# Seven of 22 gate and up pairs as seven block products, three-pass scores in the mLSTM, and another order in the banded attention

## The reference, cut to what matters

```python
def swiglu(x, wg, wu, wd):
    return (jax.nn.silu(x @ wg) * (x @ wu)) @ wd
```

```python
wts = jnp.exp(dmat - m_out[..., None])          # dmat holds a triangular mask
s_qk = jnp.einsum('bhcjd,bhcsd->bhcjs', q, k) * wts
num = jnp.einsum('bhcjs,bhcsv->bhcjv', s_qk, v) + ...
```

```python
s = s - slopes[:, :, None, None] * dist
pe = jnp.exp(s - m)
attn = pe / (jnp.sum(pe, axis=-1, keepdims=True) + jnp.exp(sink_l - m))
```

## Time and profile before

| | us |
|---|---|
| median of 3 runs | 3383.4 |
| lowest and highest run | 3382.89, 3386.52 |
| profiled execution | 3386.68 |
| its span on the core | 3384.6 |
| TensorE busy in it | 3327.2 |
| VectorE, ScalarE, GpSimd busy | 1828.3, 1315.1, 17.3 |

### The profile page before, as it was taken

One profiled execution on the slowest core, in us unless ns is written; L12 is line 12 of the kernel. 1 busy time (PEld: TensorE's weight loads), 2 busy tenths in 40 slices (PEclk: granted clock), 3 DMA queues, 4 the chain that ended last, 5 costly groups with the idle time before them and its releaser, 6 DMA issues.

```text
span 3384.6 us, 42860 instructions
## 1 busy us (share of the span) xinstructions
PE 3327.2 (98%) x17260; PEld 2783.2 (82%) x17260; DVE 1828.3 (54%) x2976; ACT 1315.1 (39%) x2272; POOL 17.3 (1%) x53
## 2 busy tenths in 40 slices
PE   8999999999999999999999999999999999999998
PEld 7778888888878888888888778888888888788887
DVE  5777974434886543354436367443554337674446
ACT  4554442223574322242224445222342226653233
POOL 0000000000100000000000000000000000000000
PEclk9999999999999999999999999999999999999999
DMA  3313122233201322323232202323232332023244
GB/s 139 100 57 102 63 83 98 98 102 97 88 15 63 104 96 100 106 94 99 94 106 95 81 32 82 100 95 105 94 100 94 100 106 72 32 82 107 99 143 168
DMA packets 95640, 311.94 MB, mean 92 GB/s; under 512 B 17167, under 2 KB 18709, under 8 KB 95445
## 3 DMA queue, kind: packets, MB, share of 16 engines
q1 hardware_dynamic: 92600, 305.51, 27.2%
q10 hardware_dynamic: 2844, 3.71, 0.3%
HBM read 302.88 MB, written 2.10 MB: 90 GB/s over the span
## 4 chain that ended last, share of the span: by engine, by line
PE 89%; DVE 6%; ACT 3%; issue 1%; DMA 0%; SPq 0%; DVEq 0%; ACTq 0%
PE ps L303 25%; PE ps L305 25%; PE ps L304 25%; PE ps L300 13%; DVE WL L293 1%; ACT WH L287 1%; DVE R L694 1%; DVE XL L869 0%; DVE XT L860 0%; PE ps L3137 0%; DVE XT L863 0%; ACT XH L631 0%; ACT R L629 0%; DVE S L707 0%; PE ps L2392 0%
## 5 line engine op out<-in xcount | busy, mean ns | idle before, releaser
L303 PE MATMUL ps<-XH,WH 128*128 128x512 f32 (+1 forms) x3200 | 1186.4, 371 | 19.5 <-DVE XL L869 12.1
L305 PE MATMUL ps<-XH,WL 128*128 128x512 f32 (+1 forms) x3200 | 1170.9, 366 | 0.0
L304 PE MATMUL ps<-XL,WH 128*128 128x512 f32 (+1 forms) x3200 | 1170.8, 366 | 0.0
L293 DVE TENSOR_TENSOR WL<-RAW,WH 128x1024 fp32r<-128x1024 f32 x567 | 686.2, 1224 | 287.3 <-ACT WH L287 282.8
L303 PEld LDWEIGHTS ps<-XH,WH 128*128 128x128 f32 x3200 | 606.8, 190 | 124.9 <-DVE XL L869 11.4
L305 PEld LDWEIGHTS ps<-XH,WL 128*128 128x128 f32 x3200 | 606.5, 190 | 97.4
L304 PEld LDWEIGHTS ps<-XL,WH 128*128 128x128 f32 x3200 | 607.3, 190 | 93.8 <-issue 0.2
L287 ACT ACTIVATE WH<-RAW 128x1024 fp32r<-128x1024 f32 x567 | 587.3, 1050 | 144.9 <-DMA RAW<-units 91.5
L303 PE MATMUL ps<-HH,WH 128*128 128x512 f32 (+1 forms) x990 | 362.7, 366 | 0.0
L304 PE MATMUL ps<-HL,WH 128*128 128x512 f32 (+1 forms) x990 | 361.8, 365 | 0.0
L305 PE MATMUL ps<-HH,WL 128*128 128x512 f32 (+1 forms) x990 | 361.7, 365 | 0.0
(11 more groups left out here) (596 smaller groups left out, 3221.4 us busy)
## 6 DMA issues: line engine op xcount, KB each, us to landing
RAW<-units SPq DMA_DIRECT2D x567, 512.0 KB, 3.3
da_qx<-da_qs SPq DMA_DIRECT2D x64, 64.0 KB, 2.4
XIN<-in_x ACTq DMA_DIRECT2D x2, 1024.0 KB, 6.3
out<-YT SPq DMA_DIRECT2D x8, 256.0 KB, 3.2
mb_pairf<-constants ACTq DMA_DIRECT2D x1, 512.0 KB
GB<-in_ln_g SPq DMA_DIRECT2D x1, 512.0 KB
GB<-in_ln_b SPq DMA_DIRECT2D x1, 512.0 KB
da_pi<-in_positions ACTq DMA_DIRECT2D x1, 256.0 KB, 2.9
```

The source lines that it names most:

```text
L293: nc.vector.tensor_tensor(WL[:, u % RING, :], RAW[:, u % RING, :], WH[:, u % RING, :].bitcast(F32), ALU.subtract)\
L303: nc.tensor.matmul(out, wh, xh, start=start, stop=False)
L304: nc.tensor.matmul(out, wh, xl, start=False, stop=False)
L305: return nc.tensor.matmul(out, wl, xh, start=False, stop=stop)
```

## The change: what it does

**Feed-forward.** For the pairs j = 5 to 11 of every feed-forward (`SEVEN`), the two units and the activations are seen as 2 x 2 blocks: gate and up columns, two halves of 512 input rows, two halves of 256 tokens. Seven block products (Strassen's method in Winograd's form) take the place of eight. Each is four row tiles x three matmuls of 256 tokens:

```diff
+        def seven_pe(pe, e, j):
+            ...
+            pe.wait_ge(S["sums_split"], halved(s))
+            part_pe(X, plain(u, 0), block(0, 0), True).then_inc(S["parts_done"], 1)
+            part_pe(Y, wsum(0), xsum(0), True).then_inc(S["parts_done"], 1)
+            pe.wait_ge(S["ffn_act"], kept(f, j, 1))
+            part_pe(X, wsum(1), xsum(1), False).then_inc(S["parts_done"], 1)
+            if j > SEVEN[0]:
+                pe.wait_ge(S["ffn_dve"], joined(f, j - 1, 2))
+            part_pe(Z, plain(u, 4), block(4, 0), True).then_inc(S["unit_done"], 1)
+            pe.wait_ge(S["ffn_act"], kept(f, j, 3))
+            part_pe(X, plain(u + 1, 0), xsum(2), False).then_inc(S["parts_done"], 1)
+            part_pe(Y, wsum(2), block(4, 1), False).then_inc(S["parts_done"], 1)
+            pe.wait_ge(S["ffn_act"], kept(f, j, 4))
+            part_pe(X, plain(u + 1, 4), xsum(3), False).then_inc(S["unit_done"], 1)
```

GpSimd makes the sums. Once for each feed-forward, when all of XH and XL is there, nine operations of 128 x 1024 give four sums of activation blocks; for each of the seven pairs, four operations of 128 x 512 give the sums of the weight blocks. The first of the four goes into the up unit's place in RAW, in place of half of it; the others go to WSR, of which there are two:

```diff
+                for i, j in enumerate(SEVEN):
+                    u, b = e["n0"] + 2 * j, j % 2
+                    for n in (u, u + 1):
+                        pool.wait_ge(raw_in[n % RING], 16 * (n // RING + 1))
+                    if i >= 2:
+                        pool.wait_ge(S["unit_done"], u + 2 - 4)
+                    ...
+                    own(g.tensor_tensor(u1, g1, u1, ALU.subtract), "sums_made")
+                    own(g.tensor_tensor(s2, u2, u1, ALU.subtract), "sums_made")
+                    own(g.tensor_tensor(s4, g2, s2, ALU.subtract), "sums_made")
+                    own(g.tensor_tensor(s1, s2, g1, ALU.add), "sums_made")
```

ScalarE and VectorE split the sums into high and low parts where they split the up unit: 128 x 1536 in one instruction each (`hi_to`, `lo_to`). The weights' low part of a gate unit waits for all four sums of its pair, as it overwrites RAW:

```diff
         def hi_to(act, n):
             for u in range(split["hi"], min(n, n_units)):
-                act.wait_ge(raw_in[u % RING], 16 * (u // RING + 1))
+                s = ups.get(u)
+                if s is None:
+                    act.wait_ge(raw_in[u % RING], 16 * (u // RING + 1))
+                else:
+                    act.wait_ge(S["sums_made"], made(s, 1))
                 nc.scalar.activation(WH[:, u % RING, :], RAW[:, u % RING, :], ACT.Copy).then_inc(S["wh_ready"], 1)
+                if s is not None:
+                    act.wait_ge(S["sums_made"], made(s, 4))
+                    b = SEVEN[s % NS] % 2
+                    nc.scalar.activation(WSH[b][:], WSR[b][:], ACT.Copy).then_inc(S["sums_high"], 1)
```

The units are now split four ahead of a pair instead of five, from pair 3 to pair 11 (`split_at`). The work of ScalarE and VectorE on one of the seven pairs is:

```diff
+                def seven(j):                       # ScalarE
+                    act.wait_ge(S["parts_done"], 5 * s + 1)
+                    nc.scalar.activation(sg[:, 0:HT], ps[:, b, 0:HT], ACT.Copy).then_inc(S["ffn_act"], 1)
+                    hi_to(act, split_at(e, j, 0))
+                    act.wait_ge(S["parts_done"], 5 * s + 2)
+                    nc.scalar.activation(hid[:, HT:T], ps[:, b + 1, 0:HT], ACT.Copy).then_inc(S["ffn_act"], 1)
+                    act.wait_ge(S["parts_done"], 5 * s + 3)
+                    nc.scalar.activation(sg[:, HT:T], ps[:, b, 0:HT], ACT.Copy).then_inc(S["ffn_act"], 1)
+                    hi_to(act, split_at(e, j, 1))
+                    ...
+                def seven(j):                       # VectorE
+                    lo_to(dve, split_at(e, j, 0))
+                    ...
+                    own(v.tensor_tensor(sg[:, 0:HT], sg[:, 0:HT], ps[:, 6, 0:HT], ALU.add), "ffn_dve")
+                    own(v.tensor_tensor(hid[:, HT:T], hid[:, HT:T], hid[:, 0:HT], ALU.add))
+                    own(v.tensor_tensor(sg[:, HT:T], sg[:, HT:T], ps[:, b + 1, 0:HT], ALU.add), "ffn_dve")
+                    own(v.scalar_tensor_tensor(sg, TH[:, j % 2, :], 1.0, sg, ALU.add, ALU.mult))
+                    ...
```

```diff
-            mm(ps[:, KBANK[h][i], :], K[:, h, i * P:(i + 1) * P], Q[:, h, :]).then_inc(s["st"], 1)
+            mm(out, KH[:, h, ts], QH[:, h, :], True, False)
+            mm(out, KH[:, h, ts], low_of(h, 0), False, False)
+            mm(out, low_of(h, 1)[:, ts], QH[:, h, :], False, True).then_inc(s["st"], 1)
...
-            mm(ps[:, 2, :], both, NM[:], True, True)
-            mm(ps[:, 3, :], both, NM[:], True, False)
-            for i in range(TT):
-                last = mm(ps[:, 3, i * P:(i + 1) * P], identr[:], TRI[:, d, :], False, i == 3)
-            last.then_inc(s["sp"], 1)
+            mm(ps[:, 2 + d, :], ROWS[:, row:row + 1].to_broadcast([P, P]), NM[:]).then_inc(s["sp"], 1)
```

More of the change, by code:

```diff
@@ L3296, in dve, with sums, weigh, low @@
         lo_to(dve, nk + 9)
+        def sums(p):
+            dve.wait_ge(s["pr"], 9 * p + 9)
+            own(v.tensor_tensor(RC, L[:, p % 2, :, :], ES[:, p % 2, :, :], ALU.add))
+            own(v.reciprocal(RC, RC))
+        def weigh(p, q):
+            o, _, n = BAND[order[q]]
+            for c in range(2):
+                w = PR[:, p % 2, c, o:o + n * P]
+                own(v.tensor_scalar(w, w, RC[:, q, c:c + 1], None, ALU.mult), "comb", wait=c == 1)
+        def low(p):
+            dve.wait_ge(s["ohi"], p + 1)
+            own(v.tensor_tensor(OL[:, p, :], ps[:, 0, :], OH[:, p, :].bitcast(F32), ALU.subtract), "olo")
         maxima(0, 2)
@@ L3317, in dve @@
-        dve.wait_ge(s["ohi"], NP)
-        own(v.tensor_tensor(OL[:, NP - 1, :], ps[:, 0, :], OH[:, NP - 1, :].bitcast(F32), ALU.subtract), "olo")
+        sums(0)
+        weigh(0, 0)
+        maxima(1, 0)
+        maxima(1, 1)
+        weigh(0, 1)
+        weigh(0, 2)
+        weigh(0, 3)
+        maxima(1, 2)
+        maxima(1, 3)
+        sums(1)
+        lo_to(dve, n2 + 5)
+        weigh(1, 0)
+        weigh(1, 1)
+        low(0)
+        maxima(2, 0)
+        maxima(2, 1)
+        weigh(1, 2)
@@ new lines, in dve @@
+        weigh(1, 3)
+        maxima(2, 2)
+        maxima(2, 3)
+        lo_to(dve, n2 + 6)
+        sums(2)
+        weigh(2, 0)
+        low(1)
+        maxima(3, 0)
+        maxima(3, 1)
+        weigh(2, 1)
+        weigh(2, 2)
+        weigh(2, 3)
+        maxima(3, 2)
+        maxima(3, 3)
+        lo_to(dve, n2 + 7)
+        sums(3)
+        weigh(3, 0)
+        weigh(3, 1)
+        low(2)
+        maxima(4, 0)
+        maxima(4, 1)
+        weigh(3, 2)
+        weigh(3, 3)
+        maxima(4, 2)
@@ new lines, in dve @@
+        maxima(4, 3)
+        lo_to(dve, n2 + 8)
+        sums(4)
+        weigh(4, 0)
+        weigh(4, 1)
+        maxima(5, 0)
+        maxima(5, 1)
+        low(3)
+        weigh(4, 2)
+        weigh(4, 3)
+        maxima(5, 2)
+        lo_to(dve, n2 + 9)
+        maxima(5, 3)
+        sums(5)
+        weigh(5, 0)
+        weigh(5, 1)
+        low(4)
+        maxima(6, 0)
+        maxima(6, 1)
+        weigh(5, 2)
+        weigh(5, 3)
+        maxima(6, 2)
+        maxima(6, 3)
+        lo_to(dve, n2 + 10)
@@ L3319, in dve @@
+        sums(6)
+        weigh(6, 0)
+        weigh(6, 1)
+        maxima(7, 0)
+        maxima(7, 1)
+        low(5)
+        weigh(6, 2)
+        weigh(6, 3)
+        maxima(7, 2)
+        maxima(7, 3)
+        sums(7)
+        weigh(7, 0)
+        weigh(7, 1)
+        weigh(7, 2)
+        low(6)
+        weigh(7, 3)
+        low(7)
         outproj_dve(dve, b, e, e["no"], finish, tail)
@@ L3657, in act @@
+        weights(3, 1, (2, 3))
+        backward(2, 1)
+        gate(6)
+        hi_to(act, ns + 12)
+        backward(2, 2)
+        backward(2, 3)
+        gate(7)
+        high(0)
+        normed(2, (0, 1))
+        normed(2, (2, 3))
         backward(3, 0)
+        high(1)
+        high(2)
         backward(3, 1)
-        gate(7)
-        for k in range(4):
-            high(k)
         backward(3, 2)
+        hi_to(act, ns + 13)
+        high(3)
         backward(3, 3)
-        hi_to(act, ns + 13)
```

666 lines of the change are left out of this document (472 added, 194 removed).

## The result

| | before | after |
|---|---|---|
| median of the runs (lowest to highest) | 3384.96 us (3382.89 to 3386.82, 4 runs) | 3501.57 us (3499.15 to 3502.91, 4 runs) |
| span of the profiled execution | 3384.6 | 3499.9 |
| mean granted clock of TensorE | 0.995 | 0.986 |

The changed kernel takes 1.0341 times as long, 95% interval 1.0329 to 1.0354: 117 us slower, where 3450 was forecast, 65 us slower. It lies 1.6 us above the upper end of the range, less than the spread of its four runs (3.8 us). The direction was right and both stalls are there; several prices were too low.

The account below looks back on a forecast made before the run. TensorE, 98% busy, was taken as the bound. Per feed-forward -5.5+7.9+10.6 = +13, six +78; with -11 for the mixers 3386.7+67 = 3453.7, less 3.3: 3450 us. Range of 8 in 10: 3345 to 3500.

Parts of the forecast that it names:

- Products and mixers: Seven products save 0.79 us per gate and up pair, 33.2 us in six feed-forwards; mLSTM -9, window attention -2.
- GpSimd's price: Each GpSimd sum of 128x512 takes 1.10 us, each of 1024 columns 2.0.
- Exclusion: VectorE operations with two SBUF inputs and GpSimd's cannot run together: 6.45+4.4 = 10.85 us against the pair's 10.08.
- Stall 1: Before the first changed pair, pair 5, TensorE waits 7.9 us for the weight sums' low part, in each feed-forward.
- the 7.3 us behind it: VectorE's work after GpSimd's sums, before pair 5: gate's and up's WL, two low parts, SG, the sums' low part.
- rival C: Both stalls at their upper ends and the clock with them: +131 per feed-forward, 3503 us, to 3510; chance 0.1.
- Stall 2: Before the fifth product of pairs 6 to 10, a 2.1 us wait for a ScalarE copy: 10.6 us per feed-forward.
- Rivals A and B: A: no exclusion that matters, 3379 us, chance 0.18. B: GpSimd cheap, 0.61 us a sum, 3339 us, chance 0.22.
- forecast's own upper end of 3503: The forecast's sum with the first stall at 12.3 us and the inner one at 3 a pair.

Follow-up runs that it names:

- the fills: The changed kernel with every GpSimd sum replaced by fills of about the same length, which write but read nothing: 3447.6 us, ratio 1.0186.

## Why the prediction was off in size

**Products and mixers: right.** 0.79 us a pair and -11 us were confirmed by the runs with nearly free sums (32 us for 33) and with the mixers alone (11.9).

**GpSimd's price: low.** Taken 1.10 and 2.0 us, measured alone 1.29 and 2.40 (the upper bound was about 1.3). The estimate from the Trainium skill's figure (GPSIMD Engine Reference, 3.1), 1.2 to 1.3 us, was nearer; the 1.29 us measured lies at its upper end.

**Exclusion: right, and it carries the first stall.** Its hold of GpSimd on VectorE, for which no row of before stood, is the 3.32 and 1.40 us above, and the fills take it away.

**Stall 1: 7.9 forecast, 10.4 measured, and 2.4 of clock behind it.** From GpSimd's start the forecast had pair 5 due after 34.4 us (3171.75-11.69-3125.79 = 34.3 in the last feed-forward) and the sums made after 34.9 (3160.56-3125.79 = 34.8): the sum is right, by luck, as its parts are not (low prices, too much time excluded). The failed step is the 7.3 us behind it, which took 11.1 (3160.56 to 3171.61), in each of the six feed-forwards. It assumed that GpSimd's next four sums would not get between VectorE's splits. They did, 3160.64 to 3168.84; this was named as worth 4.4 and put only into the upper end. GpSimd has nothing to wait for there (the second buffer is free), so it had to be the likely case. That the mean stall is 10.4 and not 11.7 comes from the first three feed-forwards, where pair 5 was due only after 34.7 to 37.3 us and the stall was 7.9 to 10.4. The clock was priced only in rival C.

**Stall 2: 2.1 forecast, 2.8 measured.** Right in place, count and chain. The chain from GpSimd's start to the fifth product took 8.1 us (3209.56 to 3217.67) for 7.9: sums of 6.0 instead of 4.7+0.8, but 2.1 instead of 2.4 for the high part, the copies and the semaphores. Most of the growth lies where the forecast had nothing: it let GpSimd start as the pair starts, but the chain's start is tied to TensorE's end of the pair before, and that way back is 0.4 us of the ring of 12.87. In TensorE's own count its waits are 2.28 of the 2.79 us. The other 0.5 is that a wait is counted from the end of the last matmul (0.28 us long, where the next is due after 0.12), and that the second matmul behind it comes 0.22 us later and not 0.12. The wait before the third product was in no forecast; it falls within the chain's 8.1 us and adds nothing to them.

**The whole.** Per feed-forward: stall 1 +2.5, clock +2.4, stall 2 +5 x 0.7 = 3.5; six times 8.4 are 50 us, and 3450+50 = 3500 stands against 3501.6. The mechanism was right; what failed are these three terms, two too small and one, the clock behind a stall, put at nothing. Rivals A and B fell; C, both stalls high and the clock with them (3503 to 3510, chance 0.10), was nearest, and the time also lies below the forecast's own upper end of 3503, which the range cut off at 3500. Its lower end is a slip: stalls of 4 and 1.3 add up to 6 x 5 - 11 = +19, so 3402 and not 3410.

## What to carry to other kernels

When a helper engine gets work inside a loop, write the ring down (who starts it, what comes back to that start) and compare its length with the loop's: an order changed within the ring only moves the wait. An engine that can run ahead into a free buffer will do so, also at the moment in which it is in the way. And a saving of 0.79 us a pair bears work only where an engine has room for it: three pairs apart, with their weight sums on VectorE, gained some 10 us over the mixers alone (21.6 us below the kernel before, against 11.9), while seven in a row, summed by GpSimd, lost 128.

## What the runs showed of the hardware

- Subtractions and sums of two SBUF tensors on GpSimd and VectorE held each other up in both directions (VectorE 1.22 to 3.32 us, 0.42 to 1.40; GpSimd 1.29 to 2.16, 2.40 to 3.27); GpSimd fills did not (1224 ns beside fills of 1.36 us), nor was an SG that reads PSUM held up (0.67).
- Behind 22 of 30 idle spots of 2.1 to 2.5 us, one a pair, the granted clock was down to 0.50, and the pair took 14.03 us and not 12.55; behind the other 8 it stayed at 1.00, as it did behind all 30 pairs of spots of 0.9 and 1.4 us. Behind stalls of 5.4 and 11.7 us TensorE worked some 4 us at 0.58 and 0.50.
- Matmuls of 256 columns are 0.12 us apart at the full clock and 0.21 at 0.50, those of 512 columns 0.2265 at the full clock.
